# A two-block attention kernel: four weight buffer sets in the opening, squares summed on TensorE in four 32-row parts, query sums in rows, output products inside the drain

## The chip, the core and the metric

The kernel runs on one core of a Trainium2 chip. The metric is the device time of one execution in microseconds (us); lower is better. Five engines run side by side from queues of their own: TensorE (PE in the rows; PEld is its weight load), VectorE (DVE), ScalarE (ACT), GpSimd (POOL) and SyncE (SP), of which the last here only issues DMAs. They meet at semaphores.

## The reference, cut to what matters

512 tokens of width 2048 pass through two blocks in f32. Of the first block this is what the change touches:

```python
def rmsnorm(x, g):
    return x * lax.rsqrt(jnp.mean(x * x, axis=-1, keepdims=True) + EPS) * g

h = rmsnorm(x, norm_g)                     # 512 tokens
m_k, m_v = split(rmsnorm(mem, mem_norm_g) @ w_mem_kv)   # 256 memory tokens, 1024 columns
q... = h @ w_in                            # then rmsnorm per head of 64 or 128
```

The second block projects x (four column sets), runs 8 pairs of dilated and 8 pairs of neighbourhood attention heads, gates them into y, and ends with

```python
out = y @ w_out_2
x = layer_norm(ALPHA * x + out, gain, bias)
```

## The kernel before

**Weights.** All weights are one stream of chunks of 128x2048 f32 (1 MB). SyncE loads chunk c into `w_raw[c % 2]`; ScalarE rounds it into `w_hi` (`split_hi`), VectorE writes the rest into `w_lo` (`split_lo`), and TensorE forms three products (`mm3`, L385 to L387: hi by hi, lo by hi, hi by lo), each 512 columns wide. A chunk load waits until the buffer's last `w_lo` is made (`lo_ready`), and a `w_hi` is overwritten when the chunk before it in that buffer has been used (`chunk_used`).

**Opening.** Chunks 0 to 7 multiply the memory tokens (`mem_chunk`): 4 steps of k by 2 token blocks by 3 products, 24 a chunk. Chunks 8 to 11 multiply x. Memory and x arrive in tiles among the weights. ScalarE squares each pair of tiles (`square`, 12 of 128x1024: 4 of memory, 8 of x) into two buffers, GpSimd adds them up (L2220), and `token_sums` (L587) sums over the partitions by products with two columns of ones. Roots and reciprocals follow on ScalarE and VectorE; for x the reciprocals are spread over all rows by four products (L609) into `rbc`, which scales x (`tr_scale`, `tr_hi`, `tr_lo`). ScalarE's order mixes splits and squares, so a square that waits for GpSimd holds the split behind it.

**Queries.** In the eight query groups `ssq` (L718) sums the squares of a group's heads: 8 products whose moving operand is 2 columns, after the group's first chunk. VectorE copies 16 columns out each time.

**Drain.** The second block runs a projection group beside each pair of heads: in a `pair_step` four bursts of attention (`burst`: scores L935, probabilities by values L962, turns L944) stand between four chunk products. Step 16, the last pair's, has no projection beside it. Then come the output products (`out_group`, L1076): chunks 200 to 203 by all 16 tiles of y, four token blocks. y tiles 0 to 13 are read back from DRAM into `o_raw`, rounded by ScalarE (`y_hi`) and VectorE (`part_lo`, L1979); 14 and 15 come from `o_st` (`last_hi`, `last_lo`). `o_raw` lies on the low part of the second block's input. All engines meet at a barrier, after which GpSimd's queue loads `xw`, the x of the residual sum (L2489), which `out_group(0)` needs before chunk 202.

Of the kernel before, what the change touches and what calls it, by code (L numbers as in the profile page):

```python
# [25 lines left out]
P = 128  # L26
# [35 lines left out]
for _n, _w in (("ident", 128), ("ones", 128), ("aident", 128), ("heads", 32), ("nmask", 128)):  # L62
    CON[_n] = (_at, _at + _w)
    _at += _w
N_CON = _at
BLK_START = (0, 8, 24, 32)

# [38 lines left out]
def constants():  # L106
# [5 lines left out]
    heads = np.zeros((P, 16, 2), np.float32)  # L112
    heads[:64, 0:6, 0] = 1.0
    heads[64:, 0:6, 1] = 1.0
    heads[:, 6:16, 0] = 1.0
    con[:, slice(*CON["heads"])] = heads.reshape(P, 32)
# [10 lines left out]
def build_kernel(nc, wst, xt_in, mem_in, par_in, con_in, pos_in, tab1_in, tab2_in, rpb_in, lng_in, lnb_in, out):  # L127
# [21 lines left out]
    with ctx:  # L149
# [32 lines left out]
        acc_m = sb_at("acc_m", [P, 4 * MEM], RA + 10 * KB)  # L182
        acc_x = sb_at("acc_x", [P, 2 * T], RA + 14 * KB)
        sq_r = [sb_at(f"sq_r{i}", [P, 2 * T], RA + 18 * KB + 4 * KB * i) for i in range(2)]
# [53 lines left out]
        sq_q = sb_at("sq_q", [P, 2, T], Y + 8 * KB)  # L238
        th_g = sb_at("th_g", [P, 2, T], Y + 12 * KB)
# [59 lines left out]
        w_loaded = [sem(f"w_loaded{i}") for i in range(2)]  # L299
        hi_ready, lo_ready = sem("hi_ready"), sem("lo_ready")  # L300
# [10 lines left out]
        sq_s, acc_s = sem("squares"), sem("squares_added")  # L311
# [52 lines left out]
        def split_hi(act, c, s, first=False):  # L364

            act.wait_ge(w_loaded[s], 8 * (c - s) + 16)
            if not first:
                act.wait_ge(chunk_used, c - 1)
            act.activation(w_hi[s][:], w_raw[s][:], ACT.Copy).then_inc(hi_ready, 1)  # L369
# [81 lines left out]
        PARTS_2 = ((14, 15), (0, 2), (2, 6), (6, 10), (10, 14), (15, 16))  # L451
# [24 lines left out]
        def _(sp):  # L476

            def weights(c):
                if c >= 2:
                    sp.wait_ge(lo_ready, c - 1)  # L480
                sp.dma_start(w_raw[c % 2][:], wst[c]).then_inc(w_loaded[c % 2], 16)
# [15 lines left out]
            mem_tile(2)  # L497
            mem_tile(3)
            sp.dma_start(con[:], con_in).then_inc(con_s, 16)
            weights(2)  # L500
            mem_tile(4)
            mem_tile(5)
            weights(3)
            mem_tile(6)
            mem_tile(7)
            for c, ms in ((4, (0, 1, 2)), (5, (3, 4, 5)), (6, (6, 7))):
                weights(c)
                for m in ms:
                    x_pair(m)
            for c in range(7, 10):  # L510
                weights(c)
# [14 lines left out]

            last_weights(2 * G_OUT2 + 2)
# [3 lines left out]
            for p in range(1, 5):  # L531
                k0, k1 = PARTS_2[p]
                sp.dma_start(o_raw[:, k0:k1, :], y_d[k0:k1].rearrange("n p t -> p n t")).then_inc(y_loaded[p - 1], 16)
# [19 lines left out]
        def _(pe):  # L553
# [8 lines left out]
            def wide_kt(c, kt, act, blocks, banks):  # L562

                k = 4 * (c % 4) + kt
                for b in range(blocks):
                    last = mm3(pe, bank[banks[b]][:], act[0][:, k, b * P:(b + 1) * P], act[1][:, k, b * P:(b + 1) * P],
                               wt(w_hi[c % 2], kt, 0, 512, 512), wt(w_lo[c % 2], kt, 0, 512, 512),
                               start=(k == 0), stop=(k == KT - 1))
                return last

            def mem_chunk(c):

                for kt in range(4):
                    if c < 4 and kt % 2 == 0:
                        pe.wait_ge(ml_s, 2 * c + kt // 2 + 1)
# [7 lines left out]
            def token_sums(acc, first, blocks, width, at, done):  # L583

                for b in range(blocks):
                    for n in range(1024 // width):
                        last = pe.matmul(bank[6][:, at + 2 * b:at + 2 * b + 2], acc[:, n * width + b * P:n * width + (b + 1) * P],  # L587
                                         ones[:, 0:2], start=(n == 0), stop=(n == 1024 // width - 1))
                last.then_inc(done, 1)

# [6 lines left out]
            for c in range(5):  # L597
                mem_chunk(c)
            pe.wait_ge(con_s, 16)
            pe.wait_ge(acc_s, 4)  # L600
            token_sums(acc_m, 0, 2, MEM, 0, stm_s)
            mem_chunk(5)
            mem_chunk(6)
            pe.wait_ge(acc_s, 12)
            pe.wait_ge(rs_s, 1)
            token_sums(acc_x, 4, TB, T, 8, stx_s)
            pe.wait_ge(rd_s, 1)
            for b in range(TB):
                last = pe.matmul(bank[7][:, b * P:(b + 1) * P], ones, rdiag[:, b, :], start=True, stop=True)  # L609
            last.then_inc(rb_s, 1)  # L610
            mem_chunk(7)
# [98 lines left out]
            def ssq(i, s):  # L710

                pe.wait_ge(ev_act, 2 * i + (G_Q + s))
                pe.wait_ge(qcp, 2 * i + (s + 1))
                for n_ in range(2):
                    for b in range(TB):
                        c = (b * 2 + n_) * 2
                        hd = con[:, bass.ds(4 * (2 * i) + (CON["heads"][0] + 4 * s + 2 * n_), 2)]
                        last = pe.matmul(bank[4 + s][:, c:c + 2], sq_q[:, n_, b * P:(b + 1) * P], hd,  # L718
                                         start=True, stop=True)
# [11 lines left out]
            with pe.Fori(1, 4) as i:  # L731
# [3 lines left out]
            proj(G_GATE + 1, 1)  # L735
# [25 lines left out]
            def idx_group(i, par):  # L761
# [3 lines left out]
                if first:  # L765
# [3 lines left out]
                    pe.wait_ge(qcp, 10)  # L769
# [265 lines left out]
            pair_step(16, 1, "N2", "N2", gemm=False)  # L1035
            for cc in range(2):
                burst(None, "N2", 17, cc, 0)
            pe.drain().then_inc(barrier, 1)
            pe.wait_ge(l2_ready, 128)

# [7 lines left out]
            def out_group(n_out, s, first=False):  # L1049
# [11 lines left out]
                for c in range(4):  # L1061
# [7 lines left out]
                    chunk_ready(pe, 2 * G_OUT2 + 4 * n_out + c)  # L1069
                    for kt in range(CK // 2):  # L1070
                        k = CK // 2 * c + kt
                        if first:
                            y_split(pe, k)
                        for b in range(TB):
                            for n, (l, r) in enumerate(((0, w_hi), (1, w_hi), (0, w_lo))):
                                last = pe.matmul(bank[4 * s + b][:], act_b[l][:, k, b * P:(b + 1) * P],  # L1076
                                                 wt(r[c % 2], kt, 0, 2 * GC, 2 * GC),
                                                 start=(k == 0 and n == 0 and n_out == 0), stop=(k == KT - 1 and n == 2),
                                                 skip_group_check=True)
                    last.then_inc(chunk_used, 1)  # L1080

            for n_out in range(3):
                out_group(n_out, n_out % 2, first=(n_out == 0))
# [24 lines left out]
        def _(act):  # L1108
# [23 lines left out]
            def square(q):  # L1132
# [6 lines left out]
                if q >= 2:  # L1139
                    act.wait_ge(acc_s, q - 1)  # L1140
                act.activation(sq_r[q % 2][:], src.rearrange("p a b -> p (a b)"), ACT.Square).then_inc(sq_s, 1)
# [7 lines left out]

            def tr_hi(i):  # L1150

                act.wait_ge(th_s, i + 1)
                copy(act_a[0][:, i, :], tr_h[i % 2][:]).then_inc(tt_s, 1)
# [1414 lines left out]
```

## Time and profile before

| | us |
|---|---|
| median of 3 runs (2683.64 to 2686.34) | 2684.99 |
| profiled execution, its own time | 2684.01 |
| span of its instructions | 2682.4 |
| TensorE busy | 2637.6 |
| VectorE busy | 1190.7 |
| ScalarE busy | 765.3 |
| GpSimd busy | 250.3 |

### The profile page before, as it was taken

The page shows a single profiled execution, that of the slowest core. Times are in us where ns is not written, and L with a number is a line of the kernel's source. Part 1 is how long each engine was busy: PE and PEld are TensorE (multiplying, and loading weights), DVE is VectorE, ACT ScalarE, POOL GpSimd, SP SyncE. Part 2 cuts the span into 40 slices and gives each one's busy share as a digit, 9 for nine tenths or more (in the row PEclk, how much of TensorE's full clock was granted, in tenths as well). Part 3 has the DMA queues.
Part 4 walks back from the last instruction along what each step waited for, and adds up shares of the span by engine and source line. Part 5 has one row for each costly group of instructions (what it writes and reads, how often), then busy time and mean ns, then how long its engine had stood idle before and what let it go on. Part 6 is the DMA issues. An engine that isn't in the chain of part 4 may idle for free.

```text
span 2682.4 us, 33987 instructions
## 1 busy us (share of the span) xinstructions
PE 2637.6 (98%) x12748; PEld 2122.5 (79%) x12748; DVE 1190.7 (44%) x2113; ACT 765.3 (29%) x1092; POOL 250.3 (9%) x385
## 2 busy tenths in 40 slices
PE   7999999999999999999999999999999999999998
PEld 6788888887777777888888887777777777777787
DVE  5663222223337775545554333444444434444425
ACT  5421222223323332224222222223323222323321
POOL 4111000000001100111000000000001112111000
PEclk9999999999999999999999999999999999999999
DMA  6457333333343433545544434323222222223432
GB/s 240 143 167 206 123 105 118 118 117 125 118 151 111 151 125 126 173 141 190 187 171 141 150 140 121 97 97 95 95 96 94 87 95 98 94 90 133 169 110 94
DMA packets 70547, 348.84 MB, mean 130 GB/s; under 512 B 11699, under 2 KB 11699, under 8 KB 42275
## 3 DMA queue, kind: packets, MB, share of 16 engines
q1 hardware_dynamic: 38148, 241.28, 25.9%
q0 software_dynamic: 32320, 106.46, 12.3%
q8 instruction: 55, 0.90, 0.1%
q14 instruction: 24, 0.20, 0.0%
HBM read 298.74 MB, written 50.45 MB: 130 GB/s over the span
## 4 chain that ended last, share of the span: by engine, by line
PE 95%; DVE 2%; ACT 1%; issue 1%; DMA 0%; POOL 0%; SPq 0%; DVEq 0%; ACTq 0%; POOLq 0%
PE bank L385 26%; PE bank L387 26%; PE bank L386 26%; PE bank L1076 5%; PE bank L944 2%; PE bank L962 2%; PE bank L1100 2%; PE bank L932 1%; PE bank L829 1%; DVE w_lo L374 1%; PE bank L810 1%; PE bank L935 1%; PE bank L791 1%; PE bank L758 1%; ACT w_hi L369 1%
## 5 line engine op out<-in xcount | busy, mean ns | idle before, releaser
L374 DVE TENSOR_TENSOR w_lo<-w_raw,w_hi 128x2048 fp32r<-128x2048 f32 x211 | 486.9, 2308 | 538.1 <-ACT w_hi L369 538.1
L385 PE MATMUL bank<-act_a,w_hi 128*128 128x512 f32 (+1 forms) x1672 | 659.6, 395 | 5.3 <-ACT stage L1290 3.9
L387 PE MATMUL bank<-act_a,w_hi 128*128 128x512 f32 (+1 forms) x1672 | 651.6, 390 | 0.0
L386 PE MATMUL bank<-act_a,w_lo 128*128 128x512 f32 (+1 forms) x1672 | 651.0, 389 | 0.0
L369 ACT ACTIVATE w_hi<-w_raw 128x2048 fp32r<-128x2048 f32 x210 | 401.0, 1910 | 399.8 <-PE bank L387 325.0
L385 PE MATMUL bank<-act_b,w_hi 128*128 128x512 f32 x1280 | 503.9, 394 | 1.2 <-ACT qkvg L1113 0.8
L387 PE MATMUL bank<-act_b,w_hi 128*128 128x512 f32 x1280 | 498.8, 390 | 0.0
L386 PE MATMUL bank<-act_b,w_lo 128*128 128x512 f32 x1280 | 498.3, 389 | 0.0
L385 PEld LDWEIGHTS bank<-act_a,w_hi 128*128 128x128 f32 (+1 forms) x1672 | 313.6, 188 | 79.1 <-issue 15.6
L387 PEld LDWEIGHTS bank<-act_a,w_hi 128*128 128x128 f32 (+1 forms) x1672 | 313.5, 188 | 67.2
L386 PEld LDWEIGHTS bank<-act_a,w_lo 128*128 128x128 f32 (+1 forms) x1672 | 313.9, 188 | 63.3
L385 PEld LDWEIGHTS bank<-act_b,w_hi 128*128 128x128 f32 x1280 | 240.4, 188 | 50.8 <-ACT qkvg L1113 1.2
L387 PEld LDWEIGHTS bank<-act_b,w_hi 128*128 128x128 f32 x1280 | 240.2, 188 | 50.9
L386 PEld LDWEIGHTS bank<-act_b,w_lo 128*128 128x128 f32 x1280 | 240.6, 188 | 48.2
L1401 ACT ACTIVATE prob<-prob,nmx 128x512 f32<-128x512 f32 (+1 forms) x128 | 77.8, 609 | 347.0 <-DVE nmx L1514 347.0
L1076 PE MATMUL bank<-w_hi,act_b 128*128 128x512 f32 x384 | 119.8, 394 | 0.4 <-ACT act_b L1113 0.4
L1290 ACT ACTIVATE stage<-bank,half_b 128x512 f32<-128x512 f32 x48 | 30.4, 683 | 222.1 <-PE bank L387 222.1
L2049 DVE CUSTOM_DVE_ANT_0 prob<-bank,b 128x512 f32<-128x512 f32 x64 | 41.6, 688 | 105.3 <-PE bank L932 105.2
L1514 DVE TENSOR_SCALAR prob<-prob,rden 128x256 f32<-128x256 f32 (+1 forms) x216 | 83.3, 395 | 7.1 <-DVE rden L1902 0.3
L1076 PEld LDWEIGHTS bank<-w_hi,act_b 128*128 128x128 f32 x384 | 72.5, 190 | 15.5 <-issue 0.6
L1076 PE MATMUL bank<-w_lo,act_b 128*128 128x512 f32 x192 | 75.4, 393 | 0.0
L962 PEld LDWEIGHTS bank<-prob_t,v_tok 128*64 128x64 f32 x768 | 40.7, 136 | 38.7 <-issue 35.8
(286 smaller groups left out, 2186.3 us busy)
## 6 DMA issues: line engine op xcount, KB each, us to landing
w_raw<-wst SPq DMA_DIRECT2D x215, 1024.0 KB, 4.9
mix_d<-stage POOLq DMA_DIRECT2D x24, 512.0 KB, 3.0
mixg<-mix_d POOLq DMA_DIRECT2D x8, 1536.0 KB, 6.8
b<-rows_2d POOLq DMA_DIRECT2D x16, 448.0 KB, 7.1
x_raw<-x_t SPq DMA_DIRECT2D x8, 512.0 KB, 8.3
q_d<-stage POOLq DMA_DIRECT2D x8, 512.0 KB, 3.2
g_d<-stage POOLq DMA_DIRECT2D x8, 512.0 KB, 3.2
qb<-q_d POOLq DMA_DIRECT2D x16, 256.0 KB, 3.8
```

Source lines behind the costliest of these rows:

```text
L369: act.activation(w_hi[s][:], w_raw[s][:], ACT.Copy).then_inc(hi_ready, 1)
L374: dve.tensor_tensor(w_lo[s][:], w_raw[s][:], w_hi[s][:].bitcast(F32), ALU.subtract).then_inc(lo_ready, 1)
L385: pe.matmul(out_ap, l_hi, r_hi, start=start, stop=False)
L386: pe.matmul(out_ap, l_lo, r_hi, start=False, stop=False)
L387: return pe.matmul(out_ap, l_hi, r_lo, start=False, stop=stop)
L944: last = pe.transpose(bank[T_BANK[e]][:, b * P:(b + 1) * P], prob[:, 2 * (cc % 2) + e, b * P:(b + 1) * P], ident)
L962: last = pe.matmul(bank[O_BANK][64 * e:64 * e + 64, c * P:(c + 1) * P], v_tok[par][:, vb, 64 * e:64 * e + 64], prob_t[e][:, b, :], start=( ...
L1076: last = pe.matmul(bank[4 * s + b][:], act_b[l][:, k, b * P:(b + 1) * P], wt(r[c % 2], kt, 0, 2 * GC, 2 * GC), start=(k == 0 and n == 0 an ...
L1100: last = pe.matmul(dst[:], act_b[l][:, k, b * P:(b + 1) * P], wt(r[c], kt, 0, 2 * GC, 2 * GC), start=False, stop=(k == KT - 1 and n == 2), ...
L1401: act.activation(pr, pr, ACT.Exp, bias=nmx[:, cc, e:e + 1], accum_out=rs[:, cc, e:e + 1]).then_inc(e2_ready, 1)
L1514: return dve.tensor_scalar(dst, src, by, None, ALU.mult)
L2049: ins = dve.tensor_tensor_reduce(out=dst, in0=src[:], in1=b2[2 * par + e][:, 384 - P * tb:896 - P * tb], scale=1.0, scalar=-3.4e38, op0=AL ...
```

## The change

Three parts, which share only the weight stream.

1. **Opening.** For chunks 0 to 7 there are four sets of raw, hi and lo buffers (`raw_m`, `hi_m`, `lo_m`: the two old ones and two in the region of `act_a`). The load of chunk c waits for the lo of chunk c - 4, and all loads are reordered. GpSimd adds nothing any more: ScalarE squares into four buffers, and TensorE sums each square in `row_parts`, four products of 32 output rows and 256 columns, accumulated in bank 6 or 7. They stand between the chunks in five places (sets 0 to 2, 3 and 4, 5 to 7, 8 and 9, 10 and 11). VectorE copies the 256 columns out and `token_sums` makes 6 small products of them. The spreading products stand inside chunk 7, and the hi of chunks 8 and 9 is made early.
2. **Queries.** `ssq` makes four products of 32 rows by 256 columns for a group, all eight groups accumulated in one bank, and `turn_ssq` turns the sums once.
3. **Drain.** Chunk 200 and 201's products for token blocks 0 and 1 (48 of 512 columns) stand between the bursts of step 16; blocks 2 and 3 follow after the drain. y tiles 0 to 7 are loaded and tiles 0 to 3 rounded during step 15, as soon as chunk 198 frees their room.

```diff
-        sq_r = [sb_at(f"sq_r{i}", [P, 2 * T], RA + 18 * KB + 4 * KB * i) for i in range(2)]
+        sq_r = [sb_at(f"sq_r{i}", [P, 2 * T], RA + 32 * KB + 4 * KB * i) for i in range(4)]
+        raw_m = w_raw + [sb_at(f"raw_m{i}", [P, CK * GC], RA + 8 * KB * i) for i in range(2)]
...
@@ SyncE
-                if c >= 2:
-                    sp.wait_ge(lo_ready, c - 1)
+                if c >= 4:
+                    sp.wait_ge(lo_ready, c - 3 if c < 10 else c - 1)
...
+            for c, ms in ((4, (0, 1)), (5, (2, 3)), (6, (4, 5)), (7, (6, 7))):
                 for m in ms:
                     x_pair(m)
+                weights(c)
...
+            sp.wait_ge(chunk_used, 2 * G_OUT2 - 1)
+            for n in range(2):
+                load_y(n)
             last_weights(2 * G_OUT2 + 2)
@@ TensorE
+            def row_parts(qs):
+                for q in qs:
+                    pe.wait_ge(sq_s, q + 1)
+                    q0, q1, bk = (0, 4, 6) if q < 4 else (4, 12, 7)
+                    for j in range(4):
+                        last = pe.matmul(bank[bk][32 * j:32 * j + 32, 0:256], ones[:, 0:32], sq_r[q % 4][:, 256 * j:256 * j + 256],
+                                         start=(q == q0), stop=(q == q1 - 1), skip_group_check=True)
+                    last.then_inc(sq_used, 1)
...
+            row_parts((0, 1, 2))
+            mem_chunk(3)
+            row_parts((3, 4))
+            mem_chunk(4)
+            row_parts((5, 6, 7))
+            token_sums(0, 2, 0, stm_s)
             mem_chunk(5)
+            row_parts((8, 9))
+            mem_chunk(6, lambda: row_parts((10, 11)))
+            token_sums(1, TB, 8, stx_s)
+            mem_chunk(7, spread_x)
...
             def ssq(i, s):
+                for half in range(2):
+                    for n in range(2):
+                        r = 64 * n + 32 * half
+                        last = pe.matmul(bank[4][r:r + 32, 0:256], con[:, at:at + 32], sq_q[:, n, 256 * half:256 * half + 256],
+                                         start=(j == 0), stop=(j == 7), skip_group_check=True)
...
+            burst("N2", "N2", 16, 0, 1)
+            for cc in range(1, 5):
+                if cc % 2:
+                    chunk_ready(pe, 2 * G_OUT2 + cc // 2)
+                out_products(0, 0, (cc - 1) // 2, range(2 * ((cc - 1) % 2), 2 * ((cc - 1) % 2) + 2), (0, 1))
+                if cc < 4:
+                    burst("N2", "N2", 16, cc, 1)
@@ ScalarE, squares
-                if q >= 2:
-                    act.wait_ge(acc_s, q - 1)
+                if q >= 4:
+                    act.wait_ge(sq_used, q - 3)
@@ GpSimd
-            for q in range(12):
...
-                    pool.tensor_tensor(acc[:], acc[:], sq_r[q % 2][:], ALU.add).then_inc(acc_s, 1)
```

Where the instructions stand now. First TensorE's queue in the opening, at the end of chunk 4 before (`w_hi_51` and `w_hi_52` are the two hi buffers, `mem_t` the memory tokens):

```order
L387 MATMUL bank<-w_lo_53,mem_t_61 128x512
L587 MATMUL bank<-con,acc_m 128x2 x8
L385 MATMUL bank<-w_hi_52,mem_t_61 128x512
L386 MATMUL bank<-w_hi_52,mem_t_62 128x512
L387 MATMUL bank<-w_lo_54,mem_t_61 128x512
```

and at the end of chunks 2 and 3 in the changed kernel (`hi_m_77` is the fourth hi buffer, `sq_r` the squares):

```order
L612 MATMUL bank<-sq_r_68,con 32x256 x4
L612 MATMUL bank<-sq_r_69,con 32x256 x4
L612 MATMUL bank<-sq_r_70,con 32x256 x4
L394 MATMUL bank<-hi_m_77,mem_t_61 128x512
...
L396 MATMUL bank<-lo_m_79,mem_t_61 128x512
L612 MATMUL bank<-sq_r_71,con 32x256 x4
L612 MATMUL bank<-sq_r_68,con 32x256 x4
L394 MATMUL bank<-w_hi_51,mem_t_61 128x512
```

One place with 8 narrow products has become several with four per square. Next TensorE's queue in the drain, before: the second burst of step 16, and the last rows ahead of the output products:

```order
L935 MATMUL bank<-qkvg_107,qkvg_106 128x256 x2
L962 MATMUL bank<-prob_t_135,v_tok_120 64x128
L962 MATMUL bank<-prob_t_136,v_tok_120 64x128
...
L944 MATMUL bank<-con,prob 128x128 x4
L982 MATMUL bank<-con,v_win_123 128x128 x4
L935 MATMUL bank<-qkvg_107,qkvg_106 128x256 x2
...
L962 MATMUL bank<-prob_t_136,v_tok_121 64x128
L1076 MATMUL bank<-w_hi_51,act_b_57 128x512
```

and the same burst in the changed kernel, with an output piece of 12 products ahead of it and another behind:

```order
L1097 MATMUL bank<-w_lo_53,act_b_57 128x512
L982 MATMUL bank<-qkvg_115,qkvg_114 128x256 x2
L1009 MATMUL bank<-prob_t_143,v_tok_128 64x128
L1009 MATMUL bank<-prob_t_144,v_tok_128 64x128
...
L991 MATMUL bank<-con,prob 128x128 x4
L1029 MATMUL bank<-con,v_win_131 128x128 x4
L1097 MATMUL bank<-w_hi_51,act_b_57 128x512
L1097 MATMUL bank<-w_hi_51,act_b_58 128x512
L1097 MATMUL bank<-w_lo_53,act_b_57 128x512
```

Four such pieces, 48 products, moved ahead of the end of the attention. Last VectorE's queue at the end of the drain, before (`act_b_58` is the low part of y):

```order
L1979 TENSOR_TENSOR act_b_58<-o_raw,act_b_57 128x1024
L2076 COPY prob_t_135<-bank 128x256
L2091 SCALAR_TENSOR_TENSOR o_st_138<-bank,qkvg_109 128x8x16 x4
L1979 TENSOR_TENSOR act_b_58<-o_raw,act_b_57 128x2048
L374 TENSOR_TENSOR w_lo_54<-w_raw_50,w_hi_52 128x2048
L1979 TENSOR_TENSOR act_b_58<-o_raw,act_b_57 128x2048 x2
L2099 TENSOR_TENSOR act_b_58<-o_st_138,act_b_57 128x512
```

and in the changed kernel:

```order
L2072 TENSOR_TENSOR act_b_58<-o_raw,act_b_57 128x1024
L2169 COPY prob_t_143<-bank 128x256
L2184 SCALAR_TENSOR_TENSOR o_st_146<-bank,qkvg_117 128x8x16 x4
L2072 TENSOR_TENSOR act_b_58<-o_raw,act_b_57 128x2048
L2192 TENSOR_TENSOR act_b_58<-o_st_146,act_b_57 128x512
```

The weight split and two pieces of y have moved ahead, between the bursts of step 16 and into step 15.

## Rows read from the trace of the kernel before

**Rows 1.** Section 1 of the page, engines over the whole span
```profile
PE 2637.6 (98%) x12748; PEld 2122.5 (79%) x12748; DVE 1190.7 (44%) x2113; ACT 765.3 (29%) x1092; POOL 250.3 (9%) x385
```

**Rows 2.** Waits of TensorE, 8.4 to 75.2 us: waited for: total us, times, longest
```profile
PE bank L385 <- DVE w_lo L374: 7.1, 4, 2.7
```

**Rows 3.** Stretches: length, TensorE busy us (count), granted clock, DMA share, GB/s
```profile
44.60:51.40 6.80, 6.12 (x15) 0.50 0.46 155
...
65.10:71.90 6.80, 6.43 (x18) 0.50 0.44 154
```

**Rows 4.** Timeline of TensorE, opening: start, length, what, [idle before]
```profile
18.54 0.47 PE L385 MATMUL bank<-w_hi,mem_t 128*128 128x512 f32 x1 [1.85 <-DVE w_lo L374]
...
45.27 0.76 PE L385 MATMUL bank<-w_hi,mem_t 128*128 128x512 f32 x1 [2.65 <-DVE w_lo L374]
...
61.77 1.84 PE L587 MATMUL bank<-con,acc_x 128*128 128x2 f32 x16
...
75.15 0.39 PE L385 MATMUL bank<-w_hi,act_a 128*128 128x512 f32 x1
```

**Rows 5.** Waits of all engines, 8 to 75 us
```profile
DVE w_lo L374 <- ACT w_hi L369: 14.6, 5, 6.2
...
ACT sq_r L1141 <- POOL acc_m L2220: 3.4, 1, 3.4
```

**Rows 6.** GpSimd by line, 16 to 75 us: busy us, mean ns | idle before
```profile
L2220 POOL TENSOR_TENSOR acc_x<-acc_x,sq_r 128x1024 f32<-128x1024 f32 x7 | 18.6, 2657 | 4.4 <-ACT sq_r L1141 3.7
```

**Rows 7.** Stretch 20 to 40 us: each engine's busy time, clock, DMA share, GB/s
```profile
20.00:40.00 20.00, 20.00 (x88) 16.10 (x87) 14.13 (x11) 14.27 (x16) 12.91 (x5) 1.00 0.98 374
```

**Rows 8.** Timeline of ScalarE, 13 to 14 us
```profile
13.35 0.91 ACT L1122 ACTIVATE mem_t<-mem_raw,params_sb 128x256 fp32r<-128x256 f32 x2 [2.57 <-DMA mem_raw<-mem_t]
```

**Rows 9.** Timeline of TensorE, query sums of the first query group
```profile
279.86 1.84 PE L718 MATMUL bank<-con,sq_q 128*128 128x2 f32 x16
281.56 0.49 PE L385 MATMUL bank<-act_a,w_hi 128*128 128x512 f32 x1
281.89 0.40 PE L386 MATMUL bank<-act_a,w_lo 128*128 128x512 f32 x1
```

**Rows 10.** Timeline of TensorE, one burst of attention in the second block
```profile
1880.88 0.39 PE L387 MATMUL bank<-act_b,w_hi 128*128 128x512 f32 x1
1881.20 1.13 PE L932 MATMUL bank<-qkvg,qkvg 64*128 64x512 f32 x4
1882.26 1.09 PE L962 MATMUL bank<-prob_t,v_tok 128*64 128x128 f32 x16
1883.29 1.09 PE L944 MATMUL bank<-con,prob 128*128 128x128 f32 x8
```

**Rows 11.** Timeline of TensorE, four full-width f32 products of the first block
```profile
1002.43 1.05 PE L829 MATMUL bank<-prob_t,vb 128*128 128x128 f32 x8
1003.32 0.38 PE L810 MATMUL bank<-con,prob 128*128 128x128 f32 x2
```

**Rows 12.** Stretches of the drain, TensorE alone
```profile
2471.60:2487.60 16.00, 10.43 (x93) 1.00 0.64 230
...
2489.00:2492.00 3.00, 3.00 (x8) 0.50 0.02 5
```

**Rows 13.** Timeline of TensorE after the drain
```profile
2488.45 0.93 PE L1076 MATMUL bank<-w_hi,act_b 128*128 128x512 f32 x2
...
2492.09 0.63 PE L1076 MATMUL bank<-w_hi,act_b 128*128 128x512 f32 x2
```

**Rows 14.** VectorE by line, 2471 to 2498 us
```profile
L1979 DVE TENSOR_TENSOR act_b<-o_raw,act_b 128x2048 fp32r<-128x2048 f32 (+1 forms) x4 | 8.0, 2018 | 0.7 <-ACT act_b L1113 0.7
```

**Rows 15.** Timeline, last piece on VectorE and first load on GpSimd's queue
```profile
2496.95 0.69 DVE L2099 TENSOR_TENSOR act_b<-o_st,act_b 128x512 fp32r<-128x512 f32 x1
...
2498.31 1.45 POOL L2489 DMA_DIRECT2D xw<-x_d  x2 [23.66 <-DVEq L2160]
```

**Rows 16.** DMA issues, 2471 to 2515 us: KB each, median us to landing
```profile
xw<-x_d POOLq DMA_DIRECT2D x2, 1024.0 KB, 6.2
```

More of the change, by code:

```diff
@@ L730, in _ @@
             proj(G_Q + 1, 1, lambda: ssq(0, 0))
-            with pe.Fori(1, 4) as i:
+            for i in range(1, 4):
                 proj(2 * i + G_Q, 0, lambda: ssq(i - 1, 1))
@@ L1047, in y_split, with out_products, out_group @@
                         pe.wait_ge(olo_s, len(PARTS_1) + n + 1)
-            def out_group(n_out, s, first=False):
+            def out_products(n_out, s, c, kts, blocks):
+                for kt in kts:
+                    k = CK // 2 * c + kt
+                    if n_out == 0:
+                        y_split(pe, k)
+                    for b in blocks:
+                        for n, (l, r) in enumerate(((0, w_hi), (1, w_hi), (0, w_lo))):
+                            last = pe.matmul(bank[4 * s + b][:], act_b[l][:, k, b * P:(b + 1) * P],
+                                             wt(r[c % 2], kt, 0, 2 * GC, 2 * GC),
+                                             start=(k == 0 and n == 0 and n_out == 0), stop=(k == KT - 1 and n == 2),
+                                             skip_group_check=True)
+                return last
+            burst("N2", "N2", 16, 0, 1)
+            pe.wait_ge(ev_act, evac_act(15, 1))
+            pe.wait_ge(ev_dve, evac_dve(15, 1))
+            for cc in range(1, 5):
[4 more added lines that the diff above has]
+                    burst("N2", "N2", 16, cc, 1)
+            for cc in range(2):
+                burst(None, "N2", 17, cc, 0)
+            pe.drain().then_inc(barrier, 1)
+            pe.wait_ge(l2_ready, 128)
+            def out_group(n_out, s):
                 if n_out == 1:
@@ L1068, in out_group @@
                                           start=False, stop=False, skip_group_check=True)
[L1069 to L1080, printed above, removed]
+                    early = n_out == 0 and c < 2
+                    if not early:
+                        chunk_ready(pe, 2 * G_OUT2 + 4 * n_out + c)
+                    out_products(n_out, s, c, range(CK // 2), range(2 if early else 0, TB)).then_inc(chunk_used, 1)
             for n_out in range(3):
-                out_group(n_out, n_out % 2, first=(n_out == 0))
+                out_group(n_out, n_out % 2)
             pe.wait_ge(ev_act, EV_ACT_OUT + 2)
@@ L1437, in burst_act, with pair_step @@
                     v_turned(kind, step, par, 1)
[L1439 removed]
+            def pair_step(step, par, kind, before, new, final=False):
                 for cc in range(4):
@@ L2118, in burst_dve, with pair_step @@
                     soft2_b(kind, step, cc)
-            def pair_step(step, par, kind, before, new):
+            def pair_step(step, par, kind, before, new, final=False):
                 for cc in range(4):
```

304 lines of the change are left out of this document (170 added, 134 removed).

## The prediction

> **What bounds the kernel now.** I read the page's busy times first: TensorE is busy for 98% of the span and VectorE for 44% [rows 1]. So nothing done on other engines counts unless TensorE waits for it, and any product added to TensorE is paid. Then TensorE's waits by stretch: they lie in the opening (7.1 us on weight splits from 8.4 to 75.2 us [rows 2]) and in the drain of the second block; the 2,400 us between hold almost none, so a gain there has to be products taken away. Third the granted clock by stretch: it is at its lower level, 1.2 GHz, for 6.8 us twice in the opening [rows 3] and for some 3 us after the drain [rows 12], each time after TensorE had idled or made small products.
>
> The opening's waits come from GpSimd. One add takes 2.66 us [rows 6], a square waits for the add two before it, and ScalarE's splits stand behind the squares: ScalarE waited 3.4 us for GpSimd, and VectorE 14.6 us for ScalarE's splits [rows 5], TensorE for VectorE.
>
> **The opening.** TensorE starts chunk 1 at 18.54 and the first product with x at 75.15 [rows 4]: 56.6 us. Seven chunks of 24 products at 0.227 us (the distance of dense 512-column products) are 38.1 of that. The other 18.5 are waits, small products and the lower clock. Chunk 1's own start doesn't move: it hangs on the DMA that ScalarE waits for at 13.35 [rows 8], and the loads ahead of that are the same.
>
> What the new order needs:
> - Twelve sets of four products, 32 output rows by 256 columns of f32. Full-width f32 products: 8 records of 128 columns in 0.89 us [rows 11], 0.11 each; a set has 8 records of 256 columns, so 1.78 us if its four products run one after another. Whether they do is the question of this case. In the burst of attention, 16 records of 128 columns whose outputs lie on two halves of the rows take 1.03 us [rows 10], where one after another would be 1.78: two halves run side by side, 16% above the perfect half of 0.89. Four quarters have no row. The bounds are 0.44 us (four at once) and 1.78 (none). I take 0.52, the perfect quarter plus the same 16%, since the nearest row is all but perfect.
> - Borders. Going into the burst costs 0.32 us instead of 0.23 [rows 10], the second product after small ones comes 0.33 after the first instead of 0.23 [rows 9]; with another 0.09 for the change back, 0.28 a stretch. Five stretches: 1.4.
> - So 12 x 0.52 + 1.4 = 7.6. Then 6 small products for `token_sums` at 0.23 (8 take 1.84 [rows 4]): 1.4; four spreading products at the full clock, 0.9 by [rows 11], and 0.2 of borders: 1.1; and 0.3 of waiting for the first scaled x.
>
> Sum 38.1 + 7.6 + 1.4 + 1.1 + 0.3 = 48.5, a gain of 8.1 us. It needs the splits to be early. Loads no longer wait for buffers, so DMA runs at its 374 GB/s [rows 7]: 11.8 MB stand between chunk 1 and the end of chunk 7's load, some 32 us, so chunk 7 has landed by about 45 and TensorE wants it at about 60. The tightest is chunk 2: landed about 16.7, hi after memory tile 4 until about 20.1, lo until about 22.5, wanted at 24.0. With no idle time I expect the clock to stay at 2.4 GHz.
>
> The Trainium skill bears on this twice. In "TensorE: Matmul & The Clock Gate", section on packing small matmuls, three 32-column tiles gave 2.38 times the speed; by that 79%, four give 0.56 us a set, and the sum would be 0.8 us worse over all twenty sets. "TensorEngine Tiling (Array Packing)", Key Properties, says that a change of tiling mode drains TensorE, which speaks against thirteen separate stretches; the rows put that at the 0.28 us above, which is in the sum.
>
> **The queries.** The old sums take from 279.86 to 281.56, and the next product but one is 0.10 late [rows 9]: 1.80 us a group, 14.4 for eight. New: 0.52 + 0.28 = 0.80 a group, 6.4, and 0.3 for the two turns (0.14 each by the turns' row [rows 10]). Gain 7.7 us. Bounds: 8.3 with a set at 0.44, and a loss of 2.4 with 1.78. VectorE's copies vanish; they are hidden either way under chunks of 11 us.
>
> **The drain.** From 2471.6 to 2487.6 TensorE is busy for 10.4 of 16.0 us [rows 12]: 5.6 idle. Behind it the clock halves, and the 9 products between 2488.45 and 2492.09 take 3.64 us [rows 13] instead of 2.04: 1.6. The 48 products moved in are 10.9 us in four pieces of 2.7, and a burst's chain on VectorE and ScalarE (2.4 and 1.1 us) fits under one piece. Charged against it: four more pairs of borders, 0.8; and a wait of 0.5 at the third piece, which needs y tiles 4 to 7: VectorE has in front of it the split of chunk 201 (2.3 us), the second burst and the piece of y itself (2.3; the mean over forms is 2.0 [rows 14]). Gain 5.6 + 1.6 - 0.8 - 0.5 = 5.9; bounds 7.2 and, with VectorE late at every piece, 2. What is late next is `xw`: it is issued 0.7 us after VectorE's last piece [rows 15] and lands 6.2 us later [rows 16]. After the last attention product VectorE needs about 4.2 us (gating, one piece of y, one tile), so `xw` is there some 11.1 us after it; TensorE comes to it after the 48 remaining products of chunks 200 and 201, 10.9 us. It just fits; a wait of 0 to 1 us is in the range.
>
> Reading y during step 15 costs nothing: DMA and ScalarE are idle there, and `o_raw`'s first half is free once chunk 198 is used.
>
> **Sum.** 8.1 + 7.7 + 5.9 = 21.7 us. The profiled execution took 2684.01, so 2662.3; it lies 0.98 below the median of the runs, which gives 2663.3.
>
> **Rivals.**
> - *The quarters don't overlap* (slower than before). Then a set costs 1.78, and 20 sets cost 25.2 more: 2688.5. A stretch of three sets would be 5.3 us with a quarter of the columns in use, and if the clock falls behind two of them, as it did behind small products and idle time [rows 3], 3.4 us each go on top: 2695. It turns to a loss from 1.6 us a set. For it: no row has four quarters, and each streams its own 256 columns. Against: the two halves in [rows 10] do so too and lose only 16%. 5%, of which 3 over the bound of no change.
> - *Only pairs overlap.* 0.89 a set as in the halves, 7.4 more: 2670.7. 13%.
> - *The drain stays bound by VectorE.* Its work there (four bursts at 2.4, split, three pieces of y, two tiles, two gatings, some 21 us) is as long as TensorE's 22, and it is served in order, so one late hi from ScalarE holds every burst behind it; then the barrier, and with it `xw`, is late too. It would take 4 to 6 of the 5.9 away: 2668. 16%.
> - *As forecast*: 65%, own range 2660 to 2667. The last 1% is anything else.
>
> **Range and chances.** The range takes in the forecast, the drain rival and most of the pairs: 2659 to 2673. A measurement of this kernel tells about 0.2%, 5.4 us, from no change. Faster by more: 65 + 13 + 16 less 1 = 93%. Within: 4%. Slower: 3%.
>
> **What would show it.** The narrow products' line should show sets about 0.5 us apart and no second level of the clock between 14 us and the end; 1.8 apart is the first rival, 0.9 the second. The first product with x should start near 67 us. TensorE should wait for no `lo_m` or `w_lo` after chunk 1. Each query stretch should hold TensorE for 0.8 instead of 1.8 us. In the drain the pieces should follow the bursts without idle time over 0.5 us, and VectorE's last piece should end no later than some 4 us after the last attention product. The prediction is wrong if a set costs over 1 us, if chunk 2 or 3 waits for its load, or if TensorE waits for `xw`.

## The result and the profile after

The changed kernel takes 2661.44 us (median of 4 runs, 2659.29 to 2661.86), where before took 2684.31 beside it (4 runs, 2682.37 to 2686.34): ratio on record 0.9905, 95% interval 0.9893 to 0.9917. The medians differ by 22.9 us, which is a ratio of 0.9915, inside that interval; the prediction said 21.7 less, 2663.3. Run again later the two kernels took 2660.67 (5 runs, 2659.5 to 2661.7) and 2685.94 (16 runs, 2682.42 to 2689.73), 25.3 us apart, ratio 0.9905 (0.9892 to 0.9918). So the gain is 23 to 25 us, somewhat more than forecast. Runs of before spread over 7 us and those of the changed kernel over 2.6; that turns out to matter.

The engines over the whole span, against [rows 1]:

```profile
PE 2627.4 (99%) x12762; PEld 2104.1 (79%) x12762; DVE 1183.3 (44%) x2110; ACT 766.0 (29%) x1092; POOL 219.8 (8%) x373
```

TensorE still bounds it. The waits of TensorE in the opening, 8.4 to 75 us, changed kernel (waited for, total us, times, longest), against [rows 2]:

```profile
PE bank L394 <- DVE w_lo L1612: 8.4, 1, 8.4
PE bank L394 <- DVE w_lo L1651: 2.7, 1, 2.7
PE bank L394 <- DVE act_a L1639: 0.3, 1, 0.3
```

The first is the wait before the very first product, the second the one before chunk 1. After chunk 1 there is no wait for a weight split left. TensorE's timeline of the opening, against [rows 4] (start, length, what, idle time before):

```profile
18.19 0.76 PE L394 MATMUL bank<-w_hi,mem_t 128*128 128x512 f32 x1 [2.75 <-DVE w_lo L1651]
...
30.82 1.50 PE L612 MATMUL bank<-sq_r,con 128*32 128x256 f32 x24
32.26 0.50 PE L394 MATMUL bank<-hi_m,mem_t 128*128 128x512 f32 x1
...
37.94 1.07 PE L612 MATMUL bank<-sq_r,con 128*32 128x256 f32 x16
...
44.65 1.50 PE L612 MATMUL bank<-sq_r,con 128*32 128x256 f32 x24
46.08 0.61 PE L621 MATMUL bank<-con,row_sums 128*128 128x2 f32 x4
...
60.09 0.95 PE L621 MATMUL bank<-con,row_sums 128*128 128x2 f32 x8
...
63.76 1.05 PE L629 MATMUL bank<-rdiag,con 128*128 128x128 f32 x8
...
67.87 0.47 PE L394 MATMUL bank<-w_hi,act_a 128*128 128x512 f32 x1 [0.32 <-DVE act_a L1639]
```

Three sets of four narrow products (24 records) hold TensorE for 1.44 us, from 30.82 to the next product at 32.26. The product with x starts at 67.87; it was 75.15. One thing was not forecast: chunk 1 begins at the lower clock. The clock by stretches (length, TensorE busy us (count), granted clock, DMA share, GB/s), the chunk 1 stretch, the drain, what follows it, and a place in the sparse attention, against [rows 3, 12]:

```profile
18.10:21.50 3.40, 3.31 (x8) 0.51 1.00 388
2455.80:2477.60 21.80, 21.00 (x141) 1.00 0.35 121
2477.60:2490.00 12.40, 12.38 (x61) 1.00 0.53 202
799.80:803.10 3.30, 3.30 (x11) 0.50 0.00 0
```

The drain has 0.8 us without work in 21.8, where it had 5.6 in 16.0 [rows 12], and the clock stays at 2.4 GHz behind it. A query group, against [rows 9]:

```profile
272.46 0.39 PE L396 MATMUL bank<-act_a,w_hi 128*128 128x512 f32 x1
272.78 0.64 PE L758 MATMUL bank<-sq_q,con 128*32 128x256 f32 x8
273.35 0.50 PE L394 MATMUL bank<-act_a,w_hi 128*128 128x512 f32 x1
273.68 0.39 PE L395 MATMUL bank<-act_a,w_lo 128*128 128x512 f32 x1
```

The sums take 0.57 us from start to start, where a dense sequence of `mm3` products goes on after 0.227.

**The ledger.** The same product is looked up in every trace, and the differences between such marks are compared: the start of the first product with x; the 601st to the 1601st product on `act_a` (the queries lie between); from there to the 3801st on `act_b`; and to the 4001st (the drain lies between). Below before and the changed kernel stand the experiments' kernels, told further down.

| us | profiled time | first x | queries | middle | drain | clock at 1.2 GHz from (for) |
|---|---|---|---|---|---|---|
| before | 2684.01 | 75.15 | 242.33 | 1979.22 | 66.79 | 44.6 (6.8), 65.1 (6.8), 2488.6 (3.4) |
| before, again | 2688.50 | 77.78 | 242.33 | 1980.73 | 67.09 | 44.3 (6.8), 58.0 (3.4), 68.2 (6.8), 826 (3.4), 2488 (6.8) |
| changed | 2661.46 | 67.87 | 234.21 | 1978.72 | 60.07 | 18.1 (3.4), 799.7 (3.4) |
| changed, again | 2660.97 | 65.91 | 234.21 | 1980.16 | 60.07 | 806.6 (3.4) |
| `no_opening` | 2672.18 | 78.69 | 234.21 | 1978.66 | 60.07 | 45.4 (3.4), 55.6 (6.8), 69.3 (6.8) |
| `no_queries` | 2668.26 | 66.51 | 242.33 | 1978.75 | 60.07 | 806.4 (3.4) |
| `no_drain` | 2665.14 | 66.20 | 234.21 | 1978.76 | 65.17 | none |
| `one_part` | 2681.47 | 79.00 | 243.10 | 1978.70 | 60.04 | none |
| `two_parts` | 2666.95 | 70.20 | 237.41 | 1978.67 | 60.07 | none |
| `two_sets` | 2670.37 | 75.27 | 234.21 | 1980.19 | 60.07 | 58.4 (3.4), 816 (3.4) |
| `pool_adds` | 2666.26 | 72.90 | 234.21 | 1978.38 | 60.07 | 58.0 (10.2) |
| `filler` | 2660.87 | 67.28 | 234.21 | 1978.72 | 60.07 | none |
| `quarters` | 2659.13 | 65.61 | 234.21 | 1978.60 | 60.07 | none |
| `quarters_late` | 2659.27 | 65.84 | 234.21 | 1978.54 | 60.07 | none |

(Falls at the very start and in the last layer norm, which all have, are left out.) Between the first profile of before and the first of the changed kernel the 22.55 us are 7.3 in the opening, 8.1 in the queries, 0.5 in the middle and 6.7 in the drain. The stretch from x to the queries (165.8) and the tail (153.2) are alike within 0.3 in all fourteen.

### The profile page after: what moved, and what is told of

It is laid out like the page before. It is cut to its first block, busy times and chain, and to the rows that moved or that the text cites. A ratio compares the mean times of both kernels' runs of the same rounds, so it can differ in the third digit from the quotient of the medians.

```text
span 2659.9 us, 33872 instructions
## 1 busy us (share of the span) xinstructions
PE 2627.4 (99%) x12762; PEld 2104.1 (79%) x12762; DVE 1183.3 (44%) x2110; ACT 766.0 (29%) x1092; POOL 219.8 (8%) x373
## 4 chain that ended last, share of the span: by engine, by line
PE 97%; DVE 1%; ACT 1%; issue 1%; DMA 0%; SPq 0%; ACTq 0%; DVEq 0%; POOL 0%; POOLq 0%
PE bank L394 27%; PE bank L396 26%; PE bank L395 26%; PE bank L1097 5%; PE bank L1009 2%; PE bank L991 2%; PE bank L1160 2%; PE bank L979 1%; PE bank L876 1%; PE bank L982 1%; PE bank L857 1%; PE bank L838 1%; PE bank L805 1%; PE bank L847 1%; PE bank L871 0%
## 5 line engine op out<-in xcount | busy, mean ns | idle before, releaser
L383 DVE TENSOR_TENSOR w_lo<-w_raw,w_hi 128x2048 fp32r<-128x2048 f32 x204 | 467.5, 2292 | 516.1 <-ACT w_hi L378 516.0
L378 ACT ACTIVATE w_hi<-w_raw 128x2048 fp32r<-128x2048 f32 x203 | 387.8, 1910 | 390.4 <-PE bank L396 324.2
```

Source lines behind the costliest of these rows:

```text
L383: dve.tensor_tensor(w_lo[s][:], w_raw[s][:], w_hi[s][:].bitcast(F32), ALU.subtract).then_inc(lo_ready, 1)
```

## The experiments

`no_opening`, `no_queries`, `no_drain` and `one_part` ran on one chip, where before took 2687.66 (15 runs, 2682.17 to 2689.98); all the others ran on a second one, where it took 2685.94 (16 runs) and 2686.10 (9 runs). Across the two, medians say little below 2 us, and the ledger says more.

**Do the parts add up?** Three kernels each undo one part of the change.

`no_opening`: all of part 1 undone (two buffers, GpSimd's adds, the old `token_sums`).

```diff
-    row_parts((0, 1, 2)) ... row_parts((10, 11))
+    pe.wait_ge(acc_s, 4); token_sums(acc_m, 0, 2, MEM, 0, stm_s) ...
```

> The changed kernel with its opening as before (two buffer sets, GpSimd's adds, eight-product sums); query sums and filled drain stay. Theory A, the parts add up: TensorE reaches the first product with x at 75.1 us instead of 67.9, and all of it arrives at the end: 2661.4 + 7.3 = 2668.7. Rival B, part of the 7.3 us is given back later (a wait for loads or for VectorE that a later arrival hides, as before had one of 1.7 us near 822 us that the changed kernel doesn't show): 2665 to 2667.

Measured 2672.16 (2671.44 to 2672.2), 10.7 above the changed kernel's first median and 11.5 above its second: more than either theory said. The first product with x comes at 78.69, not at 75.1, because this opening fell to the lower clock three times. The stretches of `no_opening`:

```profile
45.40:48.80 3.40, 3.40 (x8) 0.50 0.69 239
55.70:62.40 6.70, 6.09 (x14) 0.50 0.44 157
69.40:76.10 6.70, 5.57 (x14) 0.50 0.49 159
```

and TensorE's waits in it, 9.5 to 80 us:

```profile
PE bank L392 <- DVE w_lo L381: 8.7, 4, 3.6
...
PE bank L625 <- DVE rdiag L1554: 1.6, 1, 1.6
```

Four waits for the same splits as in [rows 2], 8.7 us now. Nothing of the gain is given back later: the middle is 1978.66.

`no_queries`: the old `ssq` and the copies.

```diff
-    last = pe.matmul(bank[4][r:r + 32, 0:256], con[:, at:at + 32], sq_q[:, n, 256 * half:256 * half + 256], ...)
+    last = pe.matmul(bank[4 + s][:, c:c + 2], sq_q[:, n_, b * P:(b + 1) * P], hd, start=True, stop=True)
```

> The changed kernel with the query sums as before (8 products of two columns a group and eight copies); opening and drain stay. Theory A: each of the eight groups takes 1.81 us for its sums instead of 0.77, less 0.2 for the turns: + 8.1 us, 2669.5. Rival B: VectorE's or ScalarE's work in the groups hides part of it, + 5 or less, 2666.

Measured 2670.11 (2668.26 to 2670.23). In the ledger the query stretch goes from 234.21 to 242.33, 8.12 us, and each of the two lengths is the same to 0.01 in every trace that has those sums: theory A. The medians say 8.7 to 9.4; the difference is within the spread of the runs.

`no_drain`: step 16 without products beside it, and y loaded and rounded as late as before.

```diff
-    for cc in range(1, 5): ... out_products(0, 0, (cc - 1) // 2, ..., (0, 1)); burst("N2", "N2", 16, cc, 1)
+    pair_step(16, 1, "N2", "N2", gemm=False)
```

> The changed kernel with the drain as before (step 16 without products beside it). Theory A: the eight waits of the drain come back and with them the lower clock behind it: + 6.7 us, 2668.1, of which 1.6 the clock. Rival B: the lower clock depends on where in the chip's own rhythm the drain falls, so it stays away and only 5.1 us come back: 2666.5.

Measured 2666.66 (2665.14 to 2670.68). The drain costs 65.17 instead of 60.07 in this execution, 5.1 us: rival B, to the tenth, in this execution. Its waits are those of before; the last two:

```profile
2469.18 0.66 PE L1000 MATMUL bank<-prob_t,v_tok 128*64 128x128 f32 x8 [1.25 <-DVE prob_t L2143]
2470.22 0.70 PE L1114 MATMUL bank<-w_hi,act_b 128*128 128x512 f32 x2 [0.37 <-ACT act_b L1151]
```

but no fall of the clock follows. Before had one there in both of its traces, of 3.4 us (drain 66.79) and of 6.8 us (67.09). So the drain's idle time cost 5.1 us, and 1.6 to 1.9 more in those executions in which the clock fell behind it; the runs of this kernel spread over 5.5 us. Why the clock fell in two executions and not in this one is open.

By the medians the three parts come to 10.7 to 11.5, 8.7 to 9.4 and 5.2 to 6.0 us, 24.6 to 26.9 together, and the whole change to 22.9 and 25.3: within the spread they add up.

**How far do the narrow products overlap?** `one_part` and `two_parts` leave the work alike and move the output rows: after the first set all products of a set fall on one or two groups of 32 rows, and the sums of the other rows are left out.

```diff
-    last = pe.matmul(bank[bk][32 * j:32 * j + 32, 0:256], ones[:, 0:32], ...)
+    r = 32 * j if q == q0 else 0              # two_parts: else 64 * (j % 2)
+    last = pe.matmul(bank[bk][r:r + 32, 0:256], ones[:, 0:32], ...)
```

> The changed kernel, but after the first set of each bank, which fills all rows, the four narrow products of a set all write rows 0 to 31 (10 sets in the opening, 7 of the queries; the sums are then wrong, which changes nothing in the time). Theory A, the four products of the changed kernel run side by side because they lie on four parts of the array: on one part they run one after another, 1.73 us a set instead of 0.43, so + 17 x 1.30 = 22.1, 2683.5. Rival C, what makes a set short is its narrow weights and the short output, wherever it lies: no change, 2661.4. Rival D, long stretches of narrow products let the clock fall: some 1.7 to 3.4 us more for a fall, 2687 to 2695.

> The changed kernel, but after the first set of each bank the narrow products of a set alternate between rows 0 to 31 and 64 to 95 (10 sets in the opening, 7 of the queries; the sums are then wrong, which changes nothing in the time). Theory A, the parts of the array work side by side, as many as are addressed: 0.86 us a set instead of 0.43, + 17 x 0.43 = 7.3, 2668.7, a third of what one part cost. Rival B, overlap comes by neighbouring issue and two parts do as well as four: 2661.4. Rival C, less than four parts do not overlap: as one part, 2682.

Measured: 2682.08 (2681.32 to 2683.85) and 2668.72 (2666.95 to 2669.2), against the 2683.5 and 2668.7 of theory A. By the ledger, seven query sets cost 8.89 us more on one part, 1.27 each, and 3.20 more on two, 0.46 each; ten sets of the opening cost 12.8 more than the 66.2 us of an opening without a fall, 1.28 each, and 4.0, 0.40 each. With four parts the three sets at 30.82 take 1.44 to the next product, of which 0.14 are the border that is explained further down. The same three sets in `one_part`, the first of them still on four parts:

```profile
29.26 4.07 PE L613 MATMUL bank<-sq_r,con 128*32 128x256 f32 x24
33.26 0.50 PE L394 MATMUL bank<-hi_m,mem_t 128*128 128x512 f32 x1
```

and in `two_parts`:

```profile
29.03 2.36 PE L613 MATMUL bank<-sq_r,con 128*32 128x256 f32 x24
31.32 0.50 PE L394 MATMUL bank<-hi_m,mem_t 128*128 128x512 f32 x1
```

1.44, 2.29 and 4.00 us for the same 24 records: it is the place of the output rows alone that makes them parallel, and four parts give all of the four-fold. The output rows fix both the columns of the array that a product uses and the rows of the bank that it adds to; these runs don't tell the two apart. Rival C of `one_part` falls. For D nothing speaks: there is no fall of the clock in either profile, though 4 us of narrow products stand together.

**Buffers or sums?** `two_sets` keeps TensorE's sums and gates loads and high parts as with two buffer sets.

```diff
-    if c >= 4: sp.wait_ge(lo_ready, c - 3 if c < 10 else c - 1)
+    if c >= 2: sp.wait_ge(lo_ready, c - 1)
...
-    if c >= 4: act.wait_ge(chunk_used, c - 3)
+    if c >= 2: act.wait_ge(chunk_used, c - 1)
```

> The changed kernel, but the load of chunk c waits for the low part of chunk c - 2 and its high part for the end of chunk c - 2, as if there were two sets of weight buffers; TensorE still sums the squares. Theory A, the opening's waits came from GpSimd's adds and what ScalarE had queued behind them: a second pair of buffers is worth little, first product with x at most 2 us later, 2661 to 2663.5. Theory B, they came from loads held back by two buffers: TensorE waits for low parts again, 5 us or more, 2667 and above.

Measured 2675.2 (2670.37 to 2675.99): theory A is wrong, and the size is beyond that of B, for all of the opening's gain is gone. But TensorE does not wait for low parts, as B had it, but for the one of chunk 1; its waits from 9.5 to 76 us are

```profile
PE bank L612 <- ACT sq_r L1201: 6.9, 3, 2.4
PE bank L394 <- DVE w_lo L1651: 1.3, 1, 1.3
```

It waits for squares: ScalarE's queue holds them behind a high part, and that one waits until TensorE has used the chunk two before it. ScalarE's waits for TensorE, from 8 to 70 us:

```profile
ACT hi_m L1173 <- PE bank L396: 10.5, 2, 6.0
...
ACT w_hi L1173 <- PE bank L396: 4.0, 1, 4.0
```

TensorE waits for a square that waits for TensorE. That holds for this order of ScalarE's queue; another one was not tried with two buffer sets.

`pool_adds` is the other half: four buffer sets, GpSimd's adds.

```diff
-    row_parts((0, 1, 2)); ...; token_sums(0, 2, 0, stm_s)
+    pe.wait_ge(acc_s, 4); token_sums(acc_m, 0, 2, MEM, 0, stm_s)
...
+    pool.tensor_tensor(acc[:], acc[:], sq_r[q % 2][:], ALU.add).then_inc(acc_s, 1)
```

> The changed kernel with its four sets of buffers and its order of loads, but GpSimd adds the squares again and TensorE makes 8 small products of them for the memory and 8 for x. Theory A, GpSimd's adds of 2.66 us hold the squares and with them ScalarE's splits: TensorE waits 5 us and more and the clock falls, 2666 to 2670, though TensorE has 4.5 us less to do (two times 1.84 us in place of 12 sets of 0.43, five borders of 0.34 and the small sums). Theory B, buffers were the cause: those 4.5 us are saved, 2657 to 2660.

Measured 2666.31 (2665.85 to 2667.15): theory A's number, but mostly by one wait, and not one for a split. TensorE's waits from 9.5 to 74 us:

```profile
PE bank L611 <- POOL acc_x L2303: 5.7, 1, 5.7
PE bank L395 <- DVE w_lo L1640: 3.3, 2, 2.0
```

It reaches the sums of x before GpSimd's eight adds are through, and the clock is low for 10.2 us from 58.0 on. So neither half alone is the change: against `no_opening` the buffers alone gain 5.9 us and both together 10.7 to 11.5. TensorE's sums alone gain nothing that can be told. Their median is 3.0 above that of `no_opening`, but it is from the other chip, the ratios to before overlap (0.9956, 0.9943 to 0.997, against 0.9947, 0.9933 to 0.9961), and in the profiles the first product with x comes at 75.27, earlier than the 78.69 of `no_opening`.

**The lower clock in chunk 1.** `filler` puts eleven products where TensorE idles.

```diff
     mem_chunk(0)
+    for _ in range(11):
+        pe.matmul(bank[7][:], mem_t[0][:, 0, 0:P], mem_t[0][:, 0:2, :], start=True, stop=True)
```

> The changed kernel with 11 products of 512 columns between chunk 0 and chunk 1, on the first memory rows, into a bank that is written afresh later (2.5 of the 2.9 us that TensorE idles there). Theory A, the lower clock in chunk 1 (1.65 us) follows the idle time: it is gone in each execution, first product with x at 66.3, median 2660 or less and the spread narrower. Rival B, the fall comes whatever TensorE does there, by the small start: no change, 2661.4. Rival C, the filler holds chunk 1 back: later than 18.3, 2662.

Measured 2660.96 (2660.57 to 2661.29): no fall in its profile, the four runs lie within 0.7 us, and chunk 1 starts at 19.27, a full microsecond late, which is C. The first product with x comes at 67.28, not at A's 66.3. That there is no fall says little by itself: five of the six executions without these products that were alike up to chunk 1 had none either. The unaltered kernel ran again as a control:

> The changed kernel unaltered, on the chip on which the next ones run. Theory A, the fall of the clock in chunk 1 and near 800 us is a matter of where an execution falls in the chip's own rhythm: this profiled execution has them at other places or not at all, and the first product with x starts at 66.3 where chunk 1 is spared, at 67.9 where not; runs within 2659 to 2662.5. Rival B, the falls belong to the program: both at the same places again.

2660.67 (2659.5 to 2661.7). Its chunk 1 stretch, the one near 807 us and the drain:

```profile
17.80:23.30 5.50, 5.48 (x24) 1.00 1.03 393
806.70:809.90 3.20, 3.20 (x11) 0.50 0.02 5
2477.00:2490.00 13.00, 12.91 (x66) 1.00 0.55 210
```

Chunk 1 is spared here; its first product:

```profile
17.82 0.47 PE L394 MATMUL bank<-w_hi,mem_t 128*128 128x512 f32 x1 [0.42 <-DVE w_lo L1651]
```

In the first profile TensorE got the full clock at 11.2 us, was through chunk 0 early and idled 2.75 us; here it got the full clock only at 14.7 us, its products came 0.43 us apart up to there, and it idled 0.42. In `no_drain` and `no_queries` it was 1.46 and 1.15, in before 1.85 and 2.10, and the clock held. That fits theory A for the opening, and fits the idle time as the cause; one execution with a fall doesn't prove it. Near 800 us, where a wait and small products stand together in the program, a fall came in four of the twelve executions of kernels made from the changed one and in one of two of before, so that place is rather A than B. What such a fall costs depends on where it stands. `filler` has none there and waits for VectorE:

```profile
806.56 0.66 PE L874 MATMUL bank<-prob_t,vb 128*64 128x128 f32 x8 [1.60 <-DVE prob_t L2008]
```

The first profile of the changed kernel has its fall ahead of this wait, at 799.7, and no such wait: its middle is the same 1978.72. The second has the wait and the fall behind it, at 806.6: 1980.16. And before, again:

> The kernel before, unaltered. Theory A, as above: its opening has three waits with small products behind them, so one to three falls of the clock of 3.4 or 6.8 us each, and the first product with x starts anywhere from 73.5 to 79; its runs spread over some 8 us, where those of the changed kernel spread over 3. Rival B: 75.1 again.

2686.07 (2682.92 to 2690.26), first product with x at 77.78, five falls:

```profile
44.40:51.00 6.60, 5.18 (x12) 0.50 0.48 164
58.10:61.30 3.20, 3.20 (x9) 0.50 0.77 297
68.30:75.00 6.70, 5.77 (x16) 0.50 0.45 159
826.10:829.30 3.20, 3.20 (x17) 0.50 0.00 0
2488.40:2495.00 6.60, 5.67 (x26) 0.50 0.00 0
```

Theory A: the profile on which the prediction stood was the milder one of the two.

**A better opening?** `quarters` splits chunks 1 and 2 in quarters, so that chunk 1 need not wait for 4.2 us of splits.

```diff
-    mem_hi(2); mem_split_hi(1); mem_hi(3); mem_hi(4); mem_split_hi(2); mem_hi(5)
+    for c in (1, 2):
+        quarter_hi(c, 0); mem_hi(2 * c); quarter_hi(c, 1); quarter_hi(c, 2)
+        mem_hi(2 * c + 1); quarter_hi(c, 3)
```

> The changed kernel with chunks 1 and 2 split into high and low part in quarters of 512 columns, the first quarter ahead of the memory tile, so that TensorE can begin a chunk with a quarter of it. Theory A, chunk 1 hangs on the 1.9 + 2.3 us of one whole split: it starts near 15.3 instead of 18.2 and without the lower clock, gain up to 2.9 + 1.65, first product with x near 63.5, 2657 to 2658. Rival B, the loads bound the opening: what is won at chunk 1 is waited for at chunk 2 or 3, 2660 to 2661.4.

Measured 2659.73 (2658.92 to 2661.19). Chunk 1 starts at 16.59, 1.5 us earlier than in `no_drain`, and the first product with x at 65.61, only 0.6 earlier. Of its timeline, sets 3 and 4:

```profile
34.68 0.64 PE L615 MATMUL bank<-sq_r,con 128*32 128x256 f32 x8
36.15 0.64 PE L615 MATMUL bank<-sq_r,con 128*32 128x256 f32 x8 [0.83 <-ACT sq_r L1204]
```

and ScalarE's:

```profile
33.24 1.92 ACT L1176 ACTIVATE w_hi<-w_raw 128x2048 fp32r<-128x2048 f32 x1 [3.36 <-DMA w_raw<-wst]
35.06 2.94 ACT L1204 ACTIVATE sq_r<-x_raw 128x1024 f32<-128x1024 f32 x3
```

The first square of x stands behind the high part of chunk 5, and that waits for its load: rival B, only at chunk 5. `quarters_late` moves a set behind chunk 3:

```diff
-    row_parts((0, 1, 2)); mem_chunk(3); row_parts((3, 4))
+    row_parts((0, 1)); mem_chunk(3); row_parts((2, 3, 4))
```

> Chunks 1 and 2 split in quarters as in the run named quarters, and the third set of squares moved behind chunk 3 (sets 0 and 1, then 2 to 4), since TensorE waited 0.8 us for that square there. Theory A: the wait goes and nothing comes in its place, 0.8 us less than quarters, 2658.9, first product with x near 64.8. Rival B: the memory sums or a load are late instead, 2659.7.

Measured 2659.43 (2659.02 to 2660.09), first product with x at 65.84. The wait did not go, it grew to 1.59 us: TensorE is there earlier and the square is not. Both are 1 to 2 us below the changed kernel's medians (ratios to before 0.9902 and 0.9901, against 0.9905), less than can be told apart. The square ahead of chunk 5's high part in ScalarE's queue was not tried.

## Which steps of the prediction held, and which failed

**What failed is the opening's term**, and the forecast came near in part by luck. The sum had 8.1 us for it. Between the two profiles it is 7.3, but by the medians of the kernel that undoes it, it is 10.7 to 11.5. Three steps are behind that. First, "with no idle time I expect the clock to stay at 2.4 GHz": the idle time before chunk 1 was there to be read, 1.85 us in [rows 4], the prediction itself said that this chunk's start doesn't move, and the sum had nothing for it. It was 2.75 us in the profile after, and the clock fell for 3.4 us, which cost 1.65. Second, the opening of before was read from one execution. Third, "the opening's waits come from GpSimd" is half of it: without GpSimd's adds, in `two_sets`, TensorE still waits 6.9 us for squares, behind high parts that wait for a free buffer, and with the adds but four buffer sets, in `pool_adds`, it waits 5.7 us once. The other two terms held, 7.7 forecast and 8.1 measured for the queries, 5.9 forecast and 5.1 to 6.7 measured for the drain.

**The overlap**, on which it all hung, is as forecast and better: a set costs 0.43 us (24 records in 1.30), not 0.52. The 16% that the two halves in [rows 10] lose are 0.14 us of 0.89, as much as a stretch of sets loses once at its end, whatever its length (1.44 for 1.30): most likely a border and no loss of overlap, and scaling it up with the sets was the error. Twelve sets took 5.2 us, not 6.2. The Trainium skill, "TensorE: Matmul & The Clock Gate", section on packing small matmuls, has 2.38 times the speed for three 32-column tiles, which is 79%. That loss doesn't show here; four tiles gave all of four times, by the 1.70 us that a set costs on one part.

**Borders** were 0.34 a stretch instead of 0.28 (0.09 going in, 0.14 and 0.11 coming out). They add up to 4.4 us in thirteen stretches, 0.8 more than charged. The Trainium skill, "TensorEngine Tiling (Array Packing)", Key Properties, says that a change of tiling mode drains TensorE. The trace agrees in that each stretch costs 0.34 us; that a drain is the cause, no run shows.

**The opening**: 8.1 forecast, 7.3 between the two profiles. The sets came 1.1 us cheaper, of which borders and waits took 0.6 back; chunk 1 started 0.35 earlier; against it stands 1.65 for the lower clock in chunk 1 (24 products in 7.10 us instead of 5.45). Without that fall x starts at 65.9 to 66.5, some 1 us ahead of the forecast. The larger error is on the other side: the opening of before starts x at 75.15 in the execution that was read, at 77.78 in its second profile and at 78.69 in `no_opening`, so the opening is worth 7 to 13 us by execution. All loads were there in time: no wait for `lo_m` at all.

**The queries**: 7.7 forecast, 8.12 measured. 1.81 - 0.77 = 1.04 a group, and 0.23 for the two turns.

**The drain**: 5.9 forecast, 6.7 between the profiles, of which 1.6 hang on the clock. The wait of 0.5 at the third piece did not come, and VectorE, the rival with 16%, was not late: its second piece of y ended at 2467.2, before the product that reads it at 2467.4, 0.2 us to spare. There were waits instead at the last burst and at the first output product behind it, 0.56 and 0.26 us, the first a little over the 0.5 that was to be the limit. And the cost of a wait had been read too small: eight waits of before sum to 5.65 us of idle time, but starts are late by 6.9, most likely because the first product behind a wait doesn't overlap with one before it. That pays for the borders charged. `xw` was issued at 2481.97, 0.7 us after VectorE's last piece, and its first half landed 5.4 us later, 1.3 us before its first product at 2488.62: it fitted, as worked out.

**The rest**: the middle moved by 0.5 us that the sum did not have. Of it 0.1 is a wait for VectorE, 1.74 us at 822.5 in before and 1.60 in `filler`; the rest comes in small steps up to 940 us. None of the kernels that undo one part brings it back (1978.66 to 1978.76), and its cause is open. The sum of the errors, -0.8 + 0.4 + 0.8 + 0.5, is +0.9 us against a predicted gain of 21.7; they partly cancelled, which is luck. So is it that two profiles with these falls of the clock were compared: by the later medians, 25.3 us apart, the forecast is 3.6 short.

## What to carry to other kernels

Four f32 products of 32 output rows and 256 columns on four parts of the array cost what one costs, plus about a third of a microsecond for a stretch of them; gather them into few stretches. Ask of a split improvement (more buffers, a faster sum) whether either half works alone: here the faster sum alone gained nothing that could be told, because an in-order queue tied the two. Read a stage that idles from more than one execution before pricing it, since a wait may or may not bring a fall of the clock, which cost 1.4 to 1.9 us here where no later wait hid it.

## What the runs showed of the hardware

- 24 records of 128x256 f32 with 32 output rows: 1.44 us to the next product on four parts, 2.29 on two, 4.00 on one (the first set on four).
- The clock fell for 3.4 or 6.8 us, once for 10.2 (`pool_adds`), behind idle time or small products in some executions of a kernel and not in others, with the same instructions: before 3 and 5 times, the changed kernel at 18.1 us once in six executions that were alike up to there. In a fall, products come every 0.43 us instead of 0.227.
- Stretches of 4 us with 32 output rows did not lower it in the profile of `one_part`.
- A fall at 799.7 us ahead of a wait of 1.6 us cost nothing, as the wait was gone; one at 806.6 behind that wait cost 1.4 us (middle 1978.72 and 1980.16).
- A wait cost TensorE up to 0.24 us more than the idle time that the profile gives. Timeline of TensorE in before's drain:

```profile
2484.74 0.66 PE L944 MATMUL bank<-con,prob 128*128 128x128 f32 x4
2486.64 0.66 PE L962 MATMUL bank<-prob_t,v_tok 128*64 128x128 f32 x8 [1.25 <-DVE prob_t L2076]
```

The starts are 1.90 us apart where 0.41 is usual behind a turn (2471.56 to 2471.97 in the changed kernel), so 1.49 are lost, with 1.25 listed as idle.
